# A layer step of a hybrid decoder: the last steps of the decode attention spread over the sixth weight product and into the next turn

## The chip, the core and the metric

The kernel runs on one core of a Trainium2 chip. The metric is the device time of one execution in microseconds (us), taken as the median of several runs. All products go through TensorE (PE in the profile); VectorE is DVE, ScalarE is ACT, GpSimd is POOL, and SyncE (SP) issues most DMAs. ACT issues some DMAs itself; its issuing part stands in rows as ACTq, and SP's as SPq.

## The reference, cut to what matters

One layer takes 512 prompt tokens and 8 x 8 new tokens of running sequences. A normalised input goes through one projection into two groups of heads: 8 attention heads of width 128 (sparse attention by an index; the new tokens also attend over 512 cached tokens per sequence, through paged `cache_k` and `cache_v`) and 16 state-space heads of width 64 (Mamba-2, which also updates a stored state per sequence). Output projection, residual, a gated feed-forward part and a final norm follow.

```python
def sparse_attend(q, k_sel, v_sel, idx, qpos, rel_bias):
    logits = jnp.einsum('bqhd,bqkhd->bqhk', q, k_sel).astype(jnp.float32) * (ATT_HEAD_DIM ** -0.5)
...
    p = jax.nn.softmax(logits, axis=-1)
    return jnp.einsum('bqhk,bqkhd->bqhd', p.astype(v_sel.dtype), v_sel)
...
    h_new = h * jnp.exp(last)[..., None, None] + jnp.einsum('bjh,bjhn,bjhp->bhpn', wts, Bc, xc)
...
    h = x + jnp.concatenate([att, y], axis=-1) @ w_out
```

The outputs are both groups' results after the layer, and also every new key, value, convolution tail and state.

## The kernel before, in words

Tokens lie along the free axis, 576 of them (512 prompt, 64 decode), in two halves of 288 columns. Every weight product is done in three passes (activation high part times weight high part, low times high, high times low), 16 k-tiles of 6 matmuls. Half of such a product (8 k-tiles, 48 matmuls) reads one 8-tile half of a weight unit. ACT makes the high part of the weights (`WH`, line 730 in the turns), POOL the low part (`WL`, line 734).

The middle of the program is a row of nine "turns" (`turn_pe`, `turn_act`, `turn_dve`, `turn_sp`, one per engine, each with the turn's number i). Turn i does at once: the q, k and v products of head i (six half products, `product(i, 0)` to `product(i, 5)`; i up to 7), the state-space work of head pair i (i up to 7), and the attention of head a = i - 1 (i from 1 to 8). The order on each engine is the order of the code; nothing is scheduled. Turn 8 has only attention. All small results pass through four PSUM banks, and the list `turn` gives the order in which names use each bank: whoever writes a name first waits (`tclaim`) until the name before it in the same bank has been taken out (`ttaken`).

The pieces of a turn that the change touches are these. Prompt attention: `qk0` to `qk3` are the logits of the four query blocks (DVE `logits`, ACT `exp_logits`, DVE `normal`), `pt0` to `pt3` the transposed probabilities (copied by ACT to the two halves of the tile `pt`), `pv0` to `pv3` the values (`values`, copied by ACT to `attT`). Decode attention: `lnew` are the logits over the new tokens, `S` those over the cache; `lgs` holds both, with number 4 in `exp_logits` and `normal`. The probabilities are transposed (`pts`, and in it the part `ptn` for the new tokens), `pvs` are the values over the cache `vca` (64 matmuls), DVE joins them to `attS`, PE transposes this (`ats`), ACT puts it into `attT`, and a DMA stores `attT` to the scratch `mixS` (semaphore `mixa`). State space: `xtok`, `btok`, `cb`, `su`, `y0` to `y3`, `ys`, then `us0` and `us1`, which update the decode state `h0` in place on DVE, and `fin`, the final prompt state. ACT stores `fin` (`ssm_prompt`), the head's output `xs` (`mixS`) and `h0` (`ssm_sample`, semaphore `hout`).

SP loads the inputs of the next turn's state-space work in `load_mamba(i + 1)`: eleven DMAs (`xs`, `bf`, `cf`, `sz`, twice `ea`, `abc`, `dcol`, and last the state `h0`), into the same tiles. It waits for the stores of turn i first, and PE waits for all eleven:

```python
                        sp.wait_ge(s["hout"], 16 * i + 16)
                        sp.wait_ge(s["link_s"], 4 * i + 4)
                        load_mamba(i + 1)
...
                    pe.wait_ge(s["ssm_in"], LOADS * (i + 1))
                    by_token(i, "xtok", xs)
```

After turn 8 the output projection begins; its loads wait for all stores to `mixS`. Time in a turn is counted below from the start of `product(i, 0)` at line 802 of PE.

## Time and profile before

| what | value |
|---|---|
| median of three runs | 3050.3 us (3049.33 to 3051.59) |
| the profiled execution's own time | 3047.6 us |
| its span, first to last instruction | 3045.6 us |
| PE busy | 2827.9 us, 93% of the span |
| DVE, ACT, POOL busy | 1509.6, 952.2, 548.0 us |
| mean granted clock of TensorE | 0.965 |

The span is divided by engine and line; a row of the timeline gives the start in us, the duration, the engine, the line, the operation, output and inputs, and in brackets how long the engine had been idle before it and who released it. The turns with products lie between about 575 and 1151 us, turn 8 between 1151 and 1208 us. Overlapping rows are normal on PE, where matmuls are pipelined.

### The profile page before, as it was taken

What the parts mean: (1) busy time and instruction counts of PE and PEld (TensorE: products, weight loads), DVE (VectorE), ACT (ScalarE), POOL (GpSimd) and SP (SyncE); (2) the same over time, 40 slices, a digit from 0 to 9 for tenths busy, and PEclk for the clock granted to TensorE, in tenths of its full rate; (3) what the DMA queues carried; (4) which work ended last, traced back from release to release, by engine and by line L of the source; (5) the groups of instructions that cost most, each with busy time, mean ns of one, the idle gap of its engine ahead of it and who ended that gap; (6) DMA issues with size and microseconds to landing.
All of it is one profiled execution on the core that took longest, in us unless ns stands there. A gap on an engine that the chain in (4) does not pass through costs nothing.

```text
span 3045.6 us, 49651 instructions
## 1 busy us (share of the span) xinstructions
PE 2827.9 (93%) x20713; PEld 2688.3 (88%) x20713; DVE 1509.6 (50%) x2311; ACT 952.2 (31%) x1442; POOL 548.0 (18%) x230
## 2 busy tenths in 40 slices
PE   6999999689999996997799999999999999999997
PEld 5887898577777773997799999999999999999997
DVE  3312599444444443213767667676766733222323
ACT  4223222133333322323443434334343322121222
POOL 1222233111111110332000000000000033333331
PEclk8999999799999997998899999999999999999999
DMA  6422231455555545433123233332323352323221
GB/s 201 119 67 77 68 106 50 126 145 145 152 148 152 151 139 169 140 127 104 64 94 124 99 119 100 108 112 97 127 99 107 127 198 99 114 99 115 99 99 63
DMA packets 367372, 354.00 MB, mean 116 GB/s; under 512 B 40957, under 2 KB 321125, under 8 KB 365880
## 3 DMA queue, kind: packets, MB, share of 16 engines
q1 hardware_dynamic: 334136, 325.20, 33.7%
q10 hardware_dynamic: 33024, 25.77, 2.6%
q8 instruction: 158, 2.59, 0.3%
q14 instruction: 54, 0.44, 0.0%
HBM read 303.18 MB, written 49.13 MB: 116 GB/s over the span
## 4 chain that ended last, share of the span: by engine, by line
PE 57%; issue 32%; POOL 7%; DVE 2%; ACTq 1%; ACT 1%; POOLq 0%; DVEq 0%
PE PS L1242 32%; PE PS L1224 18%; PE PS L802 6%; POOL WL L705 4%; POOL WL L734 3%; ACTq L1286 0%; DVE XR L2282 0%; ACTq L1287 0%; DVE xo_t L2287 0%; DVE xo_x L2287 0%; DVE y_out L2357 0%; POOL WL L726 0%; ACT WRAW L1295 0%; DVE rstd L2275 0%; PE PS L817 0%
## 5 line engine op out<-in xcount | busy, mean ns | idle before, releaser
L802 PE MATMUL PS<-AH,WH 128*128 128x288 f32 (+1 forms) x2208 | 493.5, 306 | 21.0 <-DVE AL L2184 7.3
L1224 PE MATMUL PS<-H,WH 128*128 128x288 f32 x2816 | 489.5, 296 | 0.7 <-DVE us L2249 0.7
L802 PE MATMUL PS<-AL,WH 128*128 128x288 f32 (+1 forms) x2208 | 481.1, 300 | 0.0
L802 PE MATMUL PS<-AH,WL 128*128 128x288 f32 (+1 forms) x2208 | 480.1, 299 | 0.0
L724 POOL TENSOR_TENSOR WL<-WRAW,WH 128x1024 fp32r<-128x1024 f32 x88 | 213.8, 2430 | 1378.8 <-ACT WH L717 1378.8
L1224 PEld LDWEIGHTS PS<-H,WH 128*128 128x128 f32 x2816 | 414.4, 189 | 0.9 <-issue 0.9
L802 PEld LDWEIGHTS PS<-AH,WH 128*128 128x128 f32 (+1 forms) x2208 | 363.6, 193 | 44.9 <-issue 28.9
L1242 PE MATMUL PS<-xo_t,WH 128*128 128x288 f32 x1888 | 380.1, 296 | 8.6 <-ACT kept L1643 7.5
L802 PEld LDWEIGHTS PS<-AL,WH 128*128 128x128 f32 (+1 forms) x2208 | 363.9, 193 | 0.0
L802 PEld LDWEIGHTS PS<-AH,WL 128*128 128x128 f32 (+1 forms) x2208 | 363.1, 192 | 0.0
L2343 DVE TENSOR_TENSOR XD<-PS,XD 128x576 f32<-128x576 f32 x176 | 133.4, 758 | 398.8 <-PE PS L1224 398.8
L1242 PEld LDWEIGHTS PS<-xo_t,WH 128*128 128x128 f32 x1888 | 303.6, 188 | 9.0 <-issue 9.0
L1224 PE MATMUL PS<-H,WL 128*128 128x288 f32 x1408 | 301.5, 296 | 0.0
L1242 PE MATMUL PS<-xo_x,WH 128*128 128x288 f32 x1408 | 285.4, 297 | 14.3 <-DVE xo_x L2287 14.3
L1242 PE MATMUL PS<-xo_t,WL 128*128 128x288 f32 x944 | 278.4, 295 | 0.0
L2200 DVE TENSOR_TENSOR WL<-WRAW,WH 128x1024 fp32r<-128x1024 f32 x147 | 179.9, 1224 | 126.8 <-ACT WH L1635 126.8
L1242 PEld LDWEIGHTS PS<-xo_x,WH 128*128 128x128 f32 x1408 | 227.7, 190 | 14.7 <-DVE xo_x L2287 14.7
L717 ACT CAST WH<-WRAW 128x1024 fp32r<-128x1024 f32 x88 | 92.7, 1054 | 435.5 <-PE PS L1224 430.7
L1224 PEld LDWEIGHTS PS<-H,WL 128*128 128x128 f32 x1408 | 226.9, 189 | 0.0
L1242 PE MATMUL PS<-xo_x,WL 128*128 128x288 f32 x704 | 208.3, 296 | 0.0
L1242 PE MATMUL PS<-xo_t,W 128*128 128x288 f32 x1392 | 196.0, 297 | 10.4 <-DVE xo_t L2287 10.4
L705 POOL TENSOR_TENSOR WL<-WRAW,WH 128x1024 fp32r<-128x1024 f32 (+1 forms) x58 | 139.4, 2406 | 361.3 <-ACT WH L700 361.3
(353 smaller groups left out, 3796.2 us busy)
## 6 DMA issues: line engine op xcount, KB each, us to landing
WRAW<-in_w_gate SPq DMA_DIRECT2D x22, 2048.0 KB
WRAW<-in_w_up SPq DMA_DIRECT2D x22, 2048.0 KB
WRAW<-in_w_down SPq DMA_DIRECT2D x22, 2048.0 KB
WRAW<-in_w_in SPq DMA_DIRECT2D x14, 2048.0 KB, 8.4
raw<-in_w_in SPq DMA_DIRECT2D x48, 512.0 KB, 4.1
kca<-in_cache_k SPq DMA_DIRECT2D x256, 64.0 KB, 2.8
vca<-in_cache_v SPq DMA_DIRECT2D x256, 64.0 KB, 2.0
WRAW<-in_w_out SPq DMA_DIRECT2D x16, 1024.0 KB
```

The source lines that it names most:

```text
L705: nc.gpsimd.tensor_tensor(WL[:, half, :, 0:w], raw[:, 8 * half:8 * half + 8, :], WH[:, half, :, 0:w].bitcast(F32), ALU.subtract).then_inc( ...
L717: nc.scalar.copy(as_down(WH, h % 2), w_down_half((1, 0)[f % 2], h)).then_inc(s["w_hi"], 1)
L724: nc.gpsimd.tensor_tensor(as_down(WL, h % 2), w_down_half((1, 0)[f % 2], h), as_down(WH, h % 2).bitcast(F32), ALU.subtract).then_inc(s["w_ ...
L734: nc.gpsimd.tensor_tensor(WL[:, half, :, :], raw, WH[:, half, :, :].bitcast(F32), ALU.subtract).then_inc(s["w_lo"], 1)
L802: last = nc.tensor.matmul(G[gslot][0:width, h, 0:HALF], wt[:, half, k % 8, 0:width], act[:, (k + shift) % KT, h * HALF:(h + 1) * HALF], st ...
L1224: last = mm(G[(slot + t) % 2][:, h, 0:HALF], wt[:, half, 2 * k + t, :], hid[:, m, k, h * HALF:(h + 1) * HALF], start=(k == 0 and wt is WH ...
L1242: last = mm(out, wt[:, k, :], act[:, m, k, :], start=(j in (0, 1, 3) and k == 0 and wt is wh and m == 0), stop=(k == 7 and wt is wl), skip ...
L2200: tt(w_low(r), operand(up, j, r), w_high(r).bitcast(F32), ALU.subtract).then_inc(s["p_lo"], 1)
L2343: tt(two(XD[:, n, :]), G[n % 2][:, :, 0:HALF], two(XD[:, n, :]), ALU.add).then_inc(s["tile_taken"], 1)
```

## The change

The change reorders work in the turns; no instruction's size or type changes, and the count of instructions stays the same but for waits.

On PE, the small steps that stood together in the middle of `product(i, 5)` (before k-tile 12) are cut into four parts, before k-tiles 9, 11, 13 and 15. The transposes of the decode probabilities (`pts`, and now `ptn` in a bank of its own) join the last part. After the product come `pvs` and then `values(i, 3)`. The transpose `ats` moves into the next turn, behind its `product(i, 0)`; the last one has a bank use of its own, `ats_last`. `qk1` moves behind `product(i, 0)`, `qk3` behind `xtok`, and `lnew` behind `product(i, 1)`. On ACT, `exp_logits(i, 4)` comes before the copy of `pt2`; the copies of `pts` and `ptn` and the three state-space stores (now `mamba_out`) come before the copy of `pv3`; the end of the attention (now `store_att`) follows `exp_logits(i, 1)` of the next turn. On DVE, `normal(i, 4)` stands between the updates from `us0` and `us1`, and the work on `lnew` (now `new_keys`) behind `take(i, 0, qT)`. SP's order is the same.

```diff
-        turn = [("qk0", 0), ("qk1", 1), ("qk2", 0), ("qk3", 1), ("lnew", 0), ("xtok0", 2), ("xtok1", 3), ("btok0", 2), ("btok1", 3),
+        turn = [("qk0", 0), ("qk1", 1), ("ats", 3), ("qk2", 0), ("qk3", 1), ("lnew", 0), ("xtok0", 2), ("xtok1", 3), ("btok0", 2), ("btok1", 3),
                 ("ktok0", 1), ("ktok1", 0), ("cb0", 2), ("cb1", 3), ("kca0", 0), ("kca1", 1), ("su", 3), ("S", 2), ("kca2", 0), ("hTb0", 3),
                 ("kca3", 1), ("y0", 3), ("kca4", 0), ("hTb1", 3), ("kca5", 1), ("y1", 3), ("vtok0", 0), ("vtok1", 1), ("y2", 3),
                 ("kca6", 0), ("y3", 3), ("kca7", 1), ("pt0", 0), ("ys", 3), ("pt1", 0), ("pv0", 1), ("us0", 3), ("pt2", 0), ("pv1", 1), ("us1", 2),
-                ("pt3", 0), ("pv2", 1), ("fin", 3), ("pv3", 1), ("pts", 0), ("pvs", 1), ("ats", 0)]
+                ("pt3", 0), ("pv2", 1), ("fin", 3), ("pts", 0), ("ptn", 2), ("pvs", 1), ("pv3", 1)]
...
-            def product(i, n, mid=None):
+            def product(i, n, between=None):
 
                 if n % 2 == 0:
                     pe.wait_ge(s["tile_taken"], 3 * i + (28 + n // 2))
-                half_unit(pe, 6 * i + 58 + n, n % 2, (1, 0, 1)[n // 2], ready=(lambda k: mid() if k == 12 else None) if mid else None)
+                half_unit(pe, 6 * i + 58 + n, n % 2, (1, 0, 1)[n // 2], ready=(lambda k: between[k]() if k in between else None) if between else None)
...
-                    qk(i, 1)
                 if units:
                     product(i, 0)
                     if early:
@@ -1044,18 +1044,24 @@
                             product(i, n)
                         pe.wait_ge(s["h_init"], 4)
                 if att:
+                    qk(i, 1)
+                    if i >= 2:
+                        tclaim(pe, "ats", i)
+                        back_att(i, "ats")
                     qk(i, 2)
+                if mamba:
+                    pe.wait_ge(s["ssm_in"], LOADS * (i + 1))
+                    by_token(i, "xtok", xs)
+                if att:
                     qk(i, 3)
+                if units and not early:
+                    product(i, 1)
+                if att:
                     tclaim(pe, "lnew", i)
                     pe.wait_ge(s["qpad_done"], a + 1)
                     for m in range(2):
                         last = mm(bank("lnew")[:, 0:NS], qpad[:, 4 * m:4 * m + 4, :].rearrange("p b r -> p (b r)"), kT[:, NP:NT], start=(m == 0), stop=(m == 1))
...
-                def rest():
+                def rest0():
                     if att:
                         probs_t(i, 1)
                         values(i, 0)
                     if mamba:
                         update(i, 0)
+
+                def rest1():
                     if att:
                         probs_t(i, 2)
                         values(i, 1)
                     if mamba:
                         update(i, 1)
+
+                def rest2():
                     if att:
                         probs_t(i, 3)
                         values(i, 2)
+
+                def rest3():
                     if mamba:
                         tclaim(pe, "fin", i)
                         pe.wait_ge(s["hT_done"], 4 * i + 4)
                         tmade(tr(bank("fin")[:, 0:P], hT[:, 3, :], ident[:, :]), "fin")
                     if att:
-                        values(i, 3)
+                        tclaim(pe, "pts", i)
+                        pe.wait_ge(s["prob"], 5 * a + 5)
+                        for j in range(4):
+                            last = tr(bank("pts")[:, j * P:(j + 1) * P], lgs[:, j * P:(j + 1) * P], ident[:, :])
+                        tmade(last, "pts")
+                        tclaim(pe, "ptn", i)
+                        tmade(tr(bank("ptn")[0:NS, 0:P], lgs[:, NP:NT], ident[:, :]), "ptn")
                 if units:
-                    product(i, 5, rest)
+                    product(i, 5, {9: rest0, 11: rest1, 13: rest2, 15: rest3})
                 else:
-                    rest()
-                if att:
-                    tclaim(pe, "pts", i)
+                    for part in (rest0, rest1, rest2, rest3):
+                        part()
+                if att:
                     tclaim(pe, "pvs", i)
-                    pe.wait_ge(s["prob"], 5 * a + 5)
+                    tgiven(pe, "pts", i)
+                    tgiven(pe, "ptn", i)
+                    pe.wait_ge(s["vca_in"], 512 * a + 512)
                     out = bank("pvs")
-                    for j in range(4):
-                        tr(bank("pts")[:, j * P:(j + 1) * P], lgs[:, j * P:(j + 1) * P], ident[:, :])
-                    last = tr(out[0:NS, 3 * P:4 * P], lgs[:, NP:NT], ident[:, :])
-                    tmade(last, "pts")
-                    tgiven(pe, "pts", i)
-                    pe.wait_ge(s["vca_in"], 512 * a + 512)
                     for m in range(2):
                         mm(out[:, m * P:(m + 1) * P], ptn[:, :], vtok[0:NS, 4, :], start=True, stop=False)
                         for j in range(4):
                             for c in range(4):
                                 last = mm(out[32 * c:32 * c + 32, m * P:(m + 1) * P], pts[:, j, 32 * c:32 * c + 32], vca[:, 4 * m + c, j, :], start=False, stop=(j == 3))
                     tmade(last, "pvs")
-                    tclaim(pe, "ats", i)
-                    pe.wait_ge(s["att_s"], a + 1)
-                    tmade(tr(bank("ats")[:, 0:P], attS[:, :], ident[:, :]), "ats")
+                    values(i, 3)
+
+            def back_att(i, name):
+
+                pe.wait_ge(s["att_s"], i - 1)
+                tmade(tr(B[3][:, 0:P], attS[:, :], ident[:, :]), "ats")
...
+            def store_att(a):
+
+                ttaken(copy(attT[:, NP:NT].rearrange("p (m c q) -> p m c q", m=2, c=4), B[3][:, 0:P].rearrange("p (c m q) -> p m c q", c=4, m=4)[:, 0:2, :, :]), "ats")
+                if a < 7:
+                    tgiven(act, "ats", a + 2)
+                else:
+                    given(act, "ats_last")
+                act.dma_start(bass.AP(mixS.tensor, a * (P * NT), [[NT, P], [1, NT]]), attT[:, :]).then_inc(s["mixa"], 16)
+
+            def mamba_out(i):
+
+                tgiven(act, "fin", i)
+                act.dma_start(bass.AP(O["ssm_prompt"].tensor, i * (P * P), [[P, P], [1, P]]), fin).then_inc(s["finout"], 16)
+                act.wait_ge(s["y_done"], i + 1)
+                act.dma_start(bass.AP(mixS.tensor, i * (P * NT) + 8 * P * NT, [[NT, P], [1, NT]]), xs[:, :]).then_inc(s["ymix"], 16)
+                act.wait_ge(s["h_done"], 2 * i + 2)
+                act.dma_start(bass.AP(O["ssm_sample"].tensor, i * (P * P), [[P, P], [NM * DS * P, NB], [1, P]]), h0[:, :, :]).then_inc(s["hout"], 16)
...
+                    if i >= 2:
+                        twait(act, "ats", i)
+                        store_att(a - 1)
...
+                        if t == 2:
+                            exp_logits(i, 4)
                         evac(i, f"pt{t}", pt[:, t % 2, 0:(t + 1) * P], bank(f"pt{t}")[:, 0:(t + 1) * P])
+                        if t == 3:
+                            evac(i, "pts", pt[:, 0, :], bank("pts")[:, :])
+                            evac(i, "ptn", ptn[:, :], bank("ptn")[0:NS, 0:P])
+                            if mamba:
+                                mamba_out(i)
                         evac(i, f"pv{t}", attT[:, t * P:(t + 1) * P], bank(f"pv{t}")[:, 0:P])
                         if t == 2 and mamba:
                             if later:
                                 act.wait_ge(s["finout"], 16 * i)
                             evac(i, "fin", fin, bank("fin")[:, 0:P])
...
+                def new_keys():
+
...
+                if att:
+                    new_keys()
...
+                        if att and g == 0:
+                            normal(i, 4)
```

The order of PE's instructions at the end of a turn and the start of the next, before (names as in the code; `lg` and `lgs` are the prompt and decode probabilities, and rows of the weight products have AH and WH):

```order
L1188 MATMUL PS<-pt,vtok 128x128 x2
L1143 MATMUL PS<-ident,hT 128x128 [waits hT_done,free3]
L1188 MATMUL PS<-pt,vtok 128x128 [waits free0,free1]
L1188 MATMUL PS<-pt,vtok 128x128 x3
L802 MATMUL PS<-AH,WH 128x288 x2
...
L1156 MATMUL PS<-ident,lgs 128x128 [waits prob,free1,free0]
L1156 MATMUL PS<-ident,lgs 128x128 x3
L1157 MATMUL PS<-ident,lgs 64x128
L1162 MATMUL PS<-vtok,ptn 128x128 [waits vca_in,free0]
...
L1169 MATMUL PS<-ident,attS 128x128 [waits att_s,free0]
L968 MATMUL PS<-kT,qT 128x128 [waits free0,tile_taken]
L968 MATMUL PS<-kT,qT 128x256 [waits free1]
```

and the same place in the change:

```order
L1205 MATMUL PS<-pt,vtok 128x128 x2
L803 MATMUL PS<-AH,WH 128x288 x2
...
L1155 MATMUL PS<-ident,hT 128x128 [waits hT_done,free3]
L1160 MATMUL PS<-ident,lgs 128x128 [waits prob,free0]
L1160 MATMUL PS<-ident,lgs 128x128 x3
L1163 MATMUL PS<-ident,lgs 64x128 [waits free2]
L803 MATMUL PS<-AH,WH 128x288 x2
...
L1176 MATMUL PS<-vtok,ptn 128x128 [waits free2,vca_in,free0,free1]
...
L1205 MATMUL PS<-pt,vtok 128x128 [waits free0,free1]
L1205 MATMUL PS<-pt,vtok 128x128 x3
L969 MATMUL PS<-kT,qT 128x128 [waits free0,tile_taken]
```

Where `fin` (`hT`) stood with four k-tiles of the product behind it, it now has one, and so have the transposes of `lgs`.

ACT at the end of a turn, from the copy of `pt2` on, before:

```order
L1442 COPY pt<-PS 128x384 [waits full0,full1]
L1442 COPY attT<-PS 128x128 [waits full1]
L1442 COPY cbm<-PS 128x128 [waits full3,finout]
L1442 COPY pt<-PS 128x512 [waits full0,full1]
L1442 COPY attT<-PS 128x128 [waits full1]
L1563 DMA ssm_prompt<-cbm 128x128 [waits free3]
L1565 DMA mixS<-xs 128x576 [waits y_done]
L1452 ACTIVATE lgs,stat<-lgs,stat 128x576 [waits nmax]
L1570 DMA ssm_sample<-h_108 128x8x128 [waits h_done]
L1573 COPY ptn<-PS 64x128 [waits full0]
L1574 COPY pt<-PS 128x512
L1442 COPY attT<-PS 128x64 [waits full0]
```

and in the change:

```order
L1471 ACTIVATE lgs,stat<-lgs,stat 128x576 [waits nmax,full1]
L1461 COPY pt<-PS 128x384 [waits full0]
L1461 COPY attT<-PS 128x128 [waits full1]
L1461 COPY cbm<-PS 128x128 [waits full3,finout]
L1461 COPY pt<-PS 128x512 [waits full0,full1]
L1461 COPY pt<-PS 128x512 [waits full0]
L1461 COPY ptn<-PS 64x128 [waits full2]
L1502 DMA ssm_prompt<-cbm 128x128 [waits free3]
L1504 DMA mixS<-xs 128x576 [waits y_done]
L1506 DMA ssm_sample<-h_108 128x8x128 [waits h_done]
L1461 COPY attT<-PS 128x128 [waits full1]
```

The three stores stood behind the copy of `pv3` and stand behind the copies of `pts` and `ptn` now, which wait for PE's last part.

PE between `product(i, 0)` and `product(i, 1)`, before:

```order
L968 MATMUL PS<-kT,qT 128x384 [waits free0]
L968 MATMUL PS<-kT,qT 128x512 [waits free1]
L1052 MATMUL PS<-kT,qpad 128x64 [waits qpad_done,free0]
L1052 MATMUL PS<-kT,qpad 128x64
L977 MATMUL PS<-ident,xs 128x128 [waits free3,free2,ssm_in]
L977 MATMUL PS<-ident,xs 128x128 x3
L979 MATMUL PS<-ident,xs 64x128
```

and in the change:

```order
L969 MATMUL PS<-kT,qT 128x256 [waits free1]
L1186 MATMUL PS<-ident,attS 128x128 [waits att_s,free3]
L969 MATMUL PS<-kT,qT 128x384 [waits free0]
L978 MATMUL PS<-ident,xs 128x128 [waits free3,free2,ssm_in]
L978 MATMUL PS<-ident,xs 128x128 x3
L980 MATMUL PS<-ident,xs 64x128
L969 MATMUL PS<-kT,qT 128x512 [waits free1]
```

`qk1` and `ats` are new ahead of `xtok` (the rows with `xs`), `qk3` (128x512) is behind it, and `ats` uses bank 3 just before `xtok` does.

## Rows read from the trace of the kernel before

**Rows 1.** PE's waits over the whole run: total us, times, longest.

```profile
PE PS L1169 <- DVE stat L2161: 9.1, 8, 1.1
PE PS L1066 <- ACT btok L1442: 4.6, 8, 0.6
```

**Rows 2.** Timeline of PE, end of turn 6 and start of turn 7.

```profile
1052.08 0.85 PE L802 MATMUL PS<-AH,WH 128*128 128x288 f32 x2
...
1061.10 0.27 PE L1143 MATMUL PS<-ident,hT 128*128 128x128 f32 x1
1062.37 1.13 PE L1188 MATMUL PS<-pt,vtok 128*128 128x128 f32 x8 [0.99 <-ACT pt L1442]
1063.26 0.51 PE L802 MATMUL PS<-AH,WH 128*128 128x288 f32 x2
...
1066.52 0.60 PE L1156 MATMUL PS<-ident,lgs 128*128 128x128 f32 x4
...
1068.06 0.48 PE L1162 MATMUL PS<-vtok,ptn 64*128 64x128 f32 x2 [0.83 <-ACT pt L1574]
...
1072.81 0.89 PE L968 MATMUL PS<-kT,qT 128*128 128x128 f32 x4 [0.39 <-ACT attT L1442]
1073.36 0.61 PE L802 MATMUL PS<-AH,WH 128*128 128x288 f32 x2
```

**Rows 3.** Timeline of ACT, its issues of stores at the ends of turns 0 and 6.

```profile
594.12 0.44 ACTq L1570 DMA_DIRECT2D ssm_sample<-h  x1
...
1063.54 0.35 ACTq L1563 DMA_DIRECT2D ssm_prompt<-cbm  x1
...
1064.47 0.39 ACTq L1570 DMA_DIRECT2D ssm_sample<-h  x1
...
1067.27 0.26 ACT L1573 COPY ptn<-PS 64x128 f32<-64x128 f32 x1 [1.97 <-PE PS L1157]
```

**Rows 4.** SP: its longest wait for a DMA, and its issues after turn 6.

```profile
SPq L558 <- DMA ssm_sample<-h: 168.8, 7, 30.2
1068.16 0.33 SPq L508 DMA_DIRECT2D xs<-xcS  x1
...
1073.65 0.61 SPq L516 DMA_DIRECT2D h<-in_state_ssm  x1
```

**Rows 5.** The load of the state after turn 6, from its issue to its landing.

```profile
DMA to landing us min/median/max: 6.9/6.9/6.9
```

**Rows 6.** Timeline of PE in turn 7, from product 0 to product 1's end.

```profile
1079.92 1.66 PE L968 MATMUL PS<-kT,qT 128*128 128x384 f32 x4
1081.42 0.61 PE L1052 MATMUL PS<-kT,qpad 128*128 128x64 f32 x4
1081.87 0.60 PE L977 MATMUL PS<-ident,xs 128*128 128x128 f32 x4
...
1088.80 0.60 PE L977 MATMUL PS<-ident,bf 128*128 128x128 f32 x4
```

**Rows 7.** Timeline of DVE in turn 7, behind product 1.

```profile
1086.25 0.21 DVE L2071 SCALAR_TENSOR_TENSOR lgs<-PS,neg_s 128x64 f32<-128x64 f32 x1
...
1090.39 2.43 DVE L2032 TENSOR_SCALAR lg<-lg,stat 128x512 f32<-128x512 f32 x1
```

**Rows 8.** PE in turn 1, and the windows view: busy us, PEclk, DMA.

```profile
610.40 0.95 PE L977 MATMUL PS<-ident,xs 128*128 128x128 f32 x4 [4.11 <-DMA h<-in_state_ssm]
...
618.96 0.60 PE L977 MATMUL PS<-ident,bf 128*128 128x128 f32 x4
610.62:614.03 3.41, 3.41 (x17) 3.37 (x16) 1.84 (x7) 2.69 (x9) 0.00 (x0) 0.50 0.85 214
```

**Rows 9.** Turn 8: logits 1 on DVE and ACT, and the last store.

```profile
1158.34 0.41 DVE L2019 SCALAR_TENSOR_TENSOR lg<-PS,neg_p 128x256 f32<-128x256 f32 x1
...
1160.12 0.19 ACT L1452 ACTIVATION_READ_ACCUMULATOR lg<-lg,stat 128x1 f32 x1
...
1208.17 0.35 ACTq L1578 DMA_DIRECT2D mixS<-attT  x1
```

More of the change, by code:

```diff
@@ L315, in nth @@
                 return first[b] + in_mamba[name]
-            if isinstance(i, int) and i == 8:
-                return first[b] + n_mamba[b] + 7 * n_all[b] + extra[b] + in_att[name]
-            return n_all[b] * i + (first[b] + n_mamba[b] - n_all[b] + in_turn[name])
+            if i == 8:
+                return first[b] + n_mamba[b] + 7 * n_all[b] + extra[b] + in_att[name] - (b == 3)
+            return n_all[b] * i + (first[b] + n_mamba[b] - n_all[b] + in_turn[name]) - (b == 3)
         first, extra = list(count), [0, 0, 1, 1]
         for b in range(4):
-            count[b] = first[b] + n_mamba[b] + 7 * n_all[b]
+            count[b] = first[b] + n_mamba[b] + 7 * n_all[b] - (b == 3)
         plan("ssy0", 2)
@@ L327, in build @@
             count[b] += n_att[b]
+        plan("ats_last", 3)
         plan("ssf0", 2)
@@ L1053, in turn_pe @@
                     tmade(last, "lnew")
-                if mamba:
-                    pe.wait_ge(s["ssm_in"], LOADS * (i + 1))
-                    by_token(i, "xtok", xs)
-                if units and not early:
-                    product(i, 1)
                 if mamba:
@@ L1200, in _ @@
             turn_pe(8, units=False, mamba=False)
+            claim(pe, "ats_last")
+            back_att(9, "ats_last")
             def norm_sum():
@@ L1556, in turn_act @@
                             evac(i, "fin", fin, bank("fin")[:, 0:P])
-                if mamba:
-                    if not att:
-                        if later:
-                            act.wait_ge(s["finout"], 16 * i)
-                        evac(i, "fin", fin, bank("fin")[:, 0:P])
-                    tgiven(act, "fin", i)
-                    act.dma_start(bass.AP(O["ssm_prompt"].tensor, i * (P * P), [[P, P], [1, P]]), fin).then_inc(s["finout"], 16)
-                    act.wait_ge(s["y_done"], i + 1)
-                    act.dma_start(bass.AP(mixS.tensor, i * (P * NT) + 8 * P * NT, [[NT, P], [1, NT]]), xs[:, :]).then_inc(s["ymix"], 16)
-                if att:
-                    exp_logits(i, 4)
-                if mamba:
-                    act.wait_ge(s["h_done"], 2 * i + 2)
-                    act.dma_start(bass.AP(O["ssm_sample"].tensor, i * (P * P), [[P, P], [NM * DS * P, NB], [1, P]]), h0[:, :, :]).then_inc(s["hout"], 16)
-                if att:
-                    twait(act, "pts", i)
-                    copy(ptn[:, :], bank("pvs")[0:NS, 3 * P:4 * P])
-                    ttaken(copy(pt[:, 0, :], bank("pts")[:, :]), "pts")
-                    evac(i, "ats", attT[:, NP:NT].rearrange("p (m c q) -> p m c q", m=2, c=4),
-                         bank("ats")[:, 0:P].rearrange("p (c m q) -> p m c q", c=4, m=4)[:, 0:2, :, :])
-                    tgiven(act, "ats", i)
-                    act.dma_start(bass.AP(mixS.tensor, a * (P * NT), [[NT, P], [1, NT]]), attT[:, :]).then_inc(s["mixa"], 16)
+                if mamba and not att:
+                    if later:
+                        act.wait_ge(s["finout"], 16 * i)
+                    evac(i, "fin", fin, bank("fin")[:, 0:P])
+                    mamba_out(i)
             turn_act(0, att=False)
@@ L1587, in _ @@
             turn_act(8, units=False, mamba=False)
+            wait(act, "ats_last")
+            store_att(7)
             def hi_p(c, h, f, down=False):
@@ L2150, in turn_dve @@
                     ls.end()
-                if att:
+                if att and not mamba:
                     normal(i, 4)
```

## The prediction

> **What bounds the kernel now.** I read the granted clock first, then PE's waits, then the timeline of one turn on PE, ACT, DVE and SP. In the turns PE has few idle places, each short and each recurring once a turn: PE waits for DVE before the transpose of `attS` (9.1 us in 8 times), and for ACT's copy of `btok` (4.6 us in 8 times) [rows 1]. The end of turn 6 holds most of it [rows 2]: 0.99 before `pv3`, 0.83 before `pvs`, 1.14 before `ats` (9.1 / 8) and 0.39 before `qk0`, 3.35 us. The change aims at these. From the start of product 0 in turn 6 to that in turn 7 a turn takes some 78 us.
>
> The second reading is who comes just behind PE. The state-space inputs of the next turn go a long way round: ACT issues the store of `h0` at 1064.47 [rows 3], SP waits for its landing (line 558, 168.8 us in 7 turns, its only long DMA wait here), begins the eleven loads at 1068.16 and issues the last one at 1073.65 [rows 4], and that lands 6.9 us later [rows 5], at 1080.55. PE's `xtok` starts at 1081.87 [rows 6]. So from the issue of the store to the last landing it is 16.1 us, and the slack is 1.3 us. In turn 1 there is none: issue at 594.12 [rows 3], `xtok` at 610.40 after 4.11 us of idle PE [rows 8], 16.3 us. The loads are what PE meets next if it gets faster or they get later; the change does both.
>
> **The change part by part, with turn 6 to 7 as the model.** Product 5 starts at 1052.08 and `fin` at 1061.10 [rows 2], 9.0 later, with four k-tiles ahead of it. Four k-tiles at full clock take 3.26 (1063.26 to 1066.52), 0.81 each. Now seven are ahead of `fin`: 3 x 0.81 = 2.4 more, so `fin` starts at 1063.5. Behind it the copies of `fin` and `pt3` come on ACT, and `pts` needs the bank of `pt3`, as `pv3` did: 1.27 later (1061.10 to 1062.37), so `pts` starts at 1064.8. That idle 0.99 stays, in a new place. `pts` and `ptn` take some 0.65, k-tile 15 covers the 0.83 that `pvs` waited for, `pvs` starts at 1066.3 and takes 2.9 (1068.06 to 1072.81 less 1.14, 0.39 and the transpose 0.3), `pv3` 0.9, `qk0` 0.2: product 0 at 1070.3 instead of 1073.36, 3.1 us earlier. That is the gain.
>
> The stores. Before, they were issued when the copy of `pv3` began, from 1063.54 to 1064.47, 0.93 from first to last [rows 3]. Now they follow the copies of `pts` and `ptn`. In the old order the first such copy began 0.75 after `pts` on PE (1066.52 [rows 2], 1067.27 [rows 3]) and waited for both; now `pts` is copied first, so the second copy begins at about 0.9: 1065.7, and the `h0` store is issued at 1066.65, 2.2 us later. The landing chain of 16.1 makes the last load land at 1082.75. SP's queue has nothing else that waits there; the K loads behind `load_mamba` move with it and are not needed before product 1 is done, so I cost them at nothing.
>
> PE reaches `xtok` after product 0 (6.56, 1073.36 to 1079.92), `qk1` 0.35, `ats` 0.15 and `qk2` 0.65: at 1078.0. It waits 4.8 us. So the 3.1 us are lost in this wait, and `xtok` comes 0.9 later than before (2.2 less the slack 1.3). `store_att` on ACT costs nothing while this wait covers it.
>
> Behind `xtok` the loop has become longer. `qk3` stood ahead of it, beside the load, and is now behind: `qk2` and `qk3` take 1.50 (1079.92 to 1081.42 [rows 6]), four of seven blocks are `qk3`'s, 0.86. `lnew` (0.45, from 1081.42 to 1081.87) goes behind product 1, where PE waited 0.59 for `btok` [rows 1]: nothing. But its work on DVE moves too. The two instructions from 1086.25 on took 0.5 [rows 7] in a place with slack. Now they stand ahead of `normal(i, 2)` and `normal(i, 3)`, of which the second was held until POOL's pass ended (2.43 us at 1090.39 for work that takes 0.5). In the new order the first is held and the second comes after it; the mask of `cb`, on which `su` and product 2 depend, comes 0.65 later. Bounds: 0 (if the order still fits) to 1.1; I take 0.65.
>
> The clock. Turn 1 shows what a long wait at `xtok` brings: the granted clock was 0.50 from 610.62 for 3.41 us [rows 8], its lower level of 1.2 GHz, after PE had been idle 4.11 us. From `xtok` to the end of product 1 it took 8.56 (610.40 to 618.96), against 6.93 (1081.87 to 1088.80 [rows 6]) without: 1.6 us. With a wait of 4.8 in every turn I expect that each time, but part of the low stretch may fall into the wait itself. Bounds 0 and 1.6, possibly twice that; I take 1.2.
>
> Sum, against the profiled execution's own 3047.6. Turn 0: `fin` has three more k-tiles ahead, so the first chain starts 2.4 later, and `xtok` of turn 1 waits for it already: +2.4. Turn 1 to 2: 0.9 + 0.86 + 0.65 = +2.4 (its wait and low clock are in the old time). Turns 2 to 6: 5 x (0.9 + 0.86 + 0.65 + 1.2) = 5 x 3.6 = +18.0. Turn 7: 0.86 + 0.65 + 1.2 behind `xtok`, and then the early end at last counts, -3.1: -0.4. Turn 8: the last store of attention (1208.17 [rows 9]) no longer stands behind `pv3` and its copy and an exp that waited for it, but `pv3` now sits before the last `ats`: 1 to 3 less, I take 1.8. Total +20.6: 3068. The profiled run lies 2.7 below the median of the runs, so the median becomes 3071.
>
> **Rivals.** (1) The forecast, late stores that hold `xtok`, with low clock: 3071, chance 0.6, its own range 3060 to 3082. (2) The same wait, but the clock stays up and DVE loses nothing: 6 x 1.2 + 7 x 0.65 = 11.8 less, 3059, chance 0.2. For it: idle places of 1 us at the end of turns cost no clock; against: turn 1. (3) Faster: the loads come in time, because the chain is shorter when it runs under a quieter time (`mixS` from `attT` no longer runs beside it). The point is 13.1 us instead of 16.1: then `xtok` is held by something else, bank 3, which `ats` uses just ahead and ACT empties only behind `exp_logits(i, 1)`. On DVE and ACT that took 1158.34 to 1160.31, 2.0 [rows 9], so `xtok` comes at 6.9 + 2.0 + 0.5 = 9.4 after product 0's start instead of 8.5. Per turn then 0.9 + 0.86 + 0.65 - 3.1 = -0.7, six times, turn 1 -2.5 at its end and -3 at its wait, turn 8 -1.8: -11.5, 3039. Turn 0's chain had no `attT` store beside it and still took 16.3, so 0.08. (4) The gain and the lateness cancel, 3050: it needs a chain some 2.5 us shorter, 0.07. (5) The low clock lasts twice as long after each wait: another 10, 3081, 0.05.
>
> The Trainium skill (DMA: Bandwidth & Descriptors, Anatomy of one DMA) fits a DMA as 2.0 us plus its bytes at 436 GB/s, for GpSimd's path. As an estimate from that page, the store of 0.52 MB would take 3.2 us and the 2.6 MB of loads 7.9, a chain of 11.1 us, and then rival (3) would hold with 3039; the trace does not agree, since its loads alone take 12.4 (1068.16 to 1080.55).
>
> **How the numbers follow.** A measurement of this kernel tells about 0.2% (6 us) from no change. Slower are (1), (2) and (5): 0.85; the same (4): 0.07; faster (3): 0.08. The range leaves out (3), (4) and the far end of (5): 3053 to 3083.
>
> **What would show it.** In the changed profile: PE waits at `xtok` for the load of `h` in every turn from 1 to 7, 4 to 6 us in turns 2 to 7; the store of `h0` is issued 14.5 after product 5 starts instead of 12.4; product 0 starts 3 us earlier relative to product 5; a clock of 0.50 right behind each wait; from one `xtok` to the next 81.5 to 82.5 us; the waits before `ats`, `pvs` and `qk0` are gone, and about 1 us is left before `pts`. I am wrong if the eleven loads land within 13 us of the store's issue, or if ACT issues the stores as early as before.

## The result: slower by 0.86%

The changed kernel took 3078.2 us in the median of four runs (3072.7 to 3079.6), the kernel before 3051.0 (3049.3 to 3052.9) beside it: a ratio of 1.0086, 95% interval 1.0068 to 1.0103. In a later comparison on another chip (e13 below) the ratio was 1.0087 (1.0074 to 1.0101). The forecast was 3071 in a range of 3053 to 3083. The execution profiled after took 3079.6 us (span 3077.5, mean granted clock 0.960), 32.0 more than the one before (3047.6, clock 0.965); the spans differ by 31.9.

PE's waits over the whole run, after (total us, times, longest):

```profile
PE PS L978 <- DMA h<-in_state_ssm: 30.3, 7, 9.3
...
PE PS L1085 <- DVE cbm L2135: 7.8, 8, 1.0
PE PS L1160 <- ACT pt L1461: 7.3, 8, 1.1
...
PE PS L1205 <- DVE attS L2197: 6.9, 8, 0.9
```

The first row is new: 30.3 us of waits at `xtok` for the load of the state, once in each of turns 1 to 7. Of the four small waits of [rows 2] the first stays, now before `pts` (line 1160); the other three are gone, and a new one has come, before `pv3` (line 1205). The row of line 1085 is the wait before `su` for DVE's mask of `cb`; it was 4.2 us before.

PE's timeline in the changed kernel, from product 5 of turn 6 to `xtok` of turn 7:

```profile
1081.58 0.63 PE L1198 MATMUL PS<-ident,lg 128*128 128x128 f32 x2
...
1092.00 0.27 PE L1155 MATMUL PS<-ident,hT 128*128 128x128 f32 x1
1093.17 0.65 PE L1160 MATMUL PS<-ident,lgs 128*128 128x128 f32 x4 [0.90 <-ACT pt L1461]
...
1098.61 1.16 PE L1205 MATMUL PS<-pt,vtok 128*128 128x128 f32 x8 [0.86 <-DVE attS L2197]
1099.60 0.39 PE L969 MATMUL PS<-kT,qT 128*128 128x128 f32 x2
...
1106.74 0.81 PE L969 MATMUL PS<-kT,qT 128*128 128x384 f32 x2
1111.02 0.90 PE L978 MATMUL PS<-ident,xs 128*128 128x128 f32 x3 [3.46 <-DMA h<-in_state_ssm]
```

ACT's store of the state, and SP's first and last load behind it:

```profile
1094.85 0.45 ACTq L1506 DMA_DIRECT2D ssm_sample<-h  x1
```

```profile
1099.02 0.33 SPq L509 DMA_DIRECT2D xs<-xcS  x1
...
1104.26 0.59 SPq L517 DMA_DIRECT2D h<-in_state_ssm  x1
```

The last load lands at 1110.97, 16.1 us after the issue of the store, as in [rows 3 to 6], and `xtok` starts at 1111.02. Before, `xtok` of this turn came 1.3 us after the last landing (0.7 to 1.6 over turns 2 to 7); now it comes with it.

`xtok` of turns 4, 5 and 6 after, and what each waited:

```profile
865.99 1.11 PE L978 MATMUL PS<-ident,xs 128*128 128x128 f32 x4 [3.80 <-DMA h<-in_state_ssm]
...
948.67 1.12 PE L978 MATMUL PS<-ident,xs 128*128 128x128 f32 x4 [4.48 <-DMA h<-in_state_ssm]
...
1029.26 1.11 PE L978 MATMUL PS<-ident,xs 128*128 128x128 f32 x4 [2.91 <-DMA h<-in_state_ssm]
```

From `xtok` to `xtok` that is 82.7 and 80.6; from turn 1 (619.33) to turn 7 (1111.02) it is 491.7 in six turns, 81.95 each. Before it was 78.6 ((1081.87 - 610.40) / 6, [rows 6, 8]). The loop adds up: from `xtok` to the issue of the store it is 65.85 us in the mean of turns 1 to 6, and from there to the next `xtok` 16.1.

Where the 31.9 us are lost, by the start of `xtok`: 8.9 by turn 1 (619.33 against 610.40), 20.2 from there to turn 7 (29.15 in all), 2.8 behind it. Turn 1's `xtok`, and the store of turn 0 that it waited for:

```profile
619.33 0.90 PE L978 MATMUL PS<-ident,xs 128*128 128x128 f32 x3 [9.31 <-DMA h<-in_state_ssm]
```

```profile
601.55 0.45 ACTq L1506 DMA_DIRECT2D ssm_sample<-h  x1
```

### The profile page after: what moved, and what is told of

Read it like the earlier page. It is cut to its first block, busy times and chain, and to the rows that moved or that the text cites. A ratio compares the mean times of both kernels' runs of the same rounds, so it can differ in the third digit from the quotient of the medians.

```text
span 3077.5 us, 49659 instructions
## 1 busy us (share of the span) xinstructions
PE 2843.4 (92%) x20713; PEld 2698.6 (88%) x20713; DVE 1485.3 (48%) x2311; ACT 951.0 (31%) x1442; POOL 547.5 (18%) x230
## 4 chain that ended last, share of the span: by engine, by line
PE 56%; issue 33%; POOL 7%; DVE 2%; ACTq 1%; ACT 1%; POOLq 0%; DVEq 0%
PE PS L1261 32%; PE PS L1243 18%; PE PS L803 6%; POOL WL L706 4%; POOL WL L735 3%; ACTq L1305 0%; DVE XR L2321 0%; ACTq L1306 0%; DVE xo_t L2326 0%; DVE xo_x L2326 0%; DVE y_out L2396 0%; POOL WL L727 0%; ACT WRAW L1314 0%; DVE rstd L2314 0%; PE PS L818 0%
## 5 line engine op out<-in xcount | busy, mean ns | idle before, releaser
L803 PE MATMUL PS<-AH,WH 128*128 128x288 f32 (+1 forms) x2208 | 501.1, 309 | 22.3 <-DVE AL L2223 7.2
L735 POOL TENSOR_TENSOR WL<-raw,WH 128x1024 fp32r<-128x1024 f32 x48 | 113.5, 2365 | 531.7 <-ACT WH L731 531.7
```

Source lines behind the costliest of these rows:

```text
L735: nc.gpsimd.tensor_tensor(WL[:, half, :, :], raw, WH[:, half, :, :].bitcast(F32), ALU.subtract).then_inc(s["w_lo"], 1)
L803: last = nc.tensor.matmul(G[gslot][0:width, h, 0:HALF], wt[:, half, k % 8, 0:width], act[:, (k + shift) % KT, h * HALF:(h + 1) * HALF], st ...
```

## The experiments

All ratios are to the kernel before on the same chip, with 95% intervals; five rounds each.

**e13, the changed kernel again.**

> The changed kernel unaltered, on the chip of these runs, as the yardstick for the runs on it: 3078 as before if its waits repeat (ratio 1.007 to 1.010); if the phase of the low clock decides which turns wait long, single runs scatter between 3068 and 3082.

Measured: 3077.6 us (3073.1 to 3080.8), ratio 1.0087 (1.0074 to 1.0101), waits at `xtok` again 30.3 us. The size of the loss repeats; it is the yardstick below.

**e1, the state's load taken off xtok's wait.**

```diff
-        LOADS = 16 * 11
+        LOADS = 16 * 10
...
                         sp.wait_ge(s["ymix"], 16 * i + 16)
-                        sp.wait_ge(s["hout"], 16 * i + 16)
                         sp.wait_ge(s["link_s"], 4 * i + 4)
                         load_mamba(i + 1)
+                        sp.wait_ge(s["hout"], 16 * i + 16)
+                        load_h(i + 1)
...
                 tclaim(pe, f"hTb{g}", i)
+                if g == 0:
+                    pe.wait_ge(s["h0_in"], 16 * (i + 1))
```

> The changed kernel with one wait taken apart: the state load h has a count of its own, which only the first transposes of h wait for, and the ten other loads of the next head no longer wait for the state's store. xtok then waits for neither. My theory (the chain store, state load holds xtok: 30.3 us of waits, and low clock behind them): the waits of L978 for the h load are gone, what is left of them is under 5 us in all; the time falls by 28 to 38 us, to 3040 to 3050. Rival (the loss is in the split of product 5 and in what follows xtok, the wait only takes the place of other waits): waits show up elsewhere, the time stays at 3065 or above.

Measured: 3054.4 us, ratio 1.0005 (0.9992 to 1.0017), 0.8% or some 25 us less than the changed kernel. The chain is the cause of nearly all of the loss. The edit does two things, and they were not parted: the state has a count of its own, and the ten other loads no longer queue behind the store. In the changed kernel the last of the ten, `dcol`, landed at 1108.92, 5.2 us after its issue and 2.05 before the state. So the count alone would spare `xtok` of turn 7 about 2.1 of its 3.46 us, an estimate from these two landings.

```profile
1103.74 0.48 SPq L516 DMA_DIRECT2D dcol<-in_d_skip  x1
```

The time only comes back to that of before, above what I expected. A wait for the loads is left in turn 1 alone (4.3 us), and another has taken the place of the rest. PE's waits in e1:

```profile
PE PS L984 <- ACT attT L1500: 9.0, 6, 1.5
```

`xtok` now waits 1.5 us for bank 3, which `ats` has used and ACT empties behind `exp_logits(i, 1)`: the next limit that the forecast's third rival named.

**e6, the same separation in the kernel before.** Edit as in e1.

> The kernel before with the state load h on a count of its own, as in the run e1_state_apart on the changed one. In the kernel before the load lands 0.2 to 1.7 us ahead of xtok, so that nothing waits for it. My theory: no change, 3050 within 0.2%, xtok to xtok 78.3 us as before. Rival (the chain bounds the kernel before too, by work that is placed behind it): 3040 or less.

Measured: 3051.5 us, ratio 0.9995 (0.9984 to 1.0006). Only turn 1 of the kernel before met the chain: its wait of 4.1 us is 0.55 in e6. That is too little to show in the time. The separation pays where the store comes late in every turn.

**e5, the kernel before with only the store late.**

```diff
-                if mamba:
-                    act.wait_ge(s["h_done"], 2 * i + 2)
-                    act.dma_start(bass.AP(O["ssm_sample"].tensor, i * (P * P), [[P, P], [NM * DS * P, NB], [1, P]]), h0[:, :, :]).then_inc(s["hout"], 16)
                 if att:
                     twait(act, "pts", i)
                     copy(ptn[:, :], bank("pvs")[0:NS, 3 * P:4 * P])
                     ttaken(copy(pt[:, 0, :], bank("pts")[:, :]), "pts")
+                if mamba:
+                    act.wait_ge(s["h_done"], 2 * i + 2)
+                    act.dma_start(bass.AP(O["ssm_sample"].tensor, i * (P * P), [[P, P], [NM * DS * P, NB], [1, P]]), h0[:, :, :]).then_inc(s["hout"], 16)
```

> The kernel before with one thing moved: the state store of turns 1 to 6 is issued behind ScalarE's copies ptn and pt, about 3.1 us later (1067.6 instead of 1064.47 in turn 6); the tail of the turn stays as it was. My theory (the chain store, state load is the bound as soon as its slack of 1.3 us is used): PE waits 1.5 to 3 us for the h load at xtok of turns 2 to 7, a low clock behind some of them; 6 turns by 1.9 to 3.1 makes 3061 to 3069. Rival (the state load is hidden and what costs in the changed kernel is its new order on PE and VectorE): no such waits, 3050 within 0.2%.

Measured: 3061.7 us against 3049.7, ratio 1.0042 (1.0029 to 1.0055). PE's waits in e5:

```profile
PE PS L977 <- DMA h<-in_state_ssm: 12.1, 7, 4.4
```

The median rose by 12 us for a late store alone, with nothing moved on PE or DVE: the rival that blamed their new order falls for this part, and the lateness is enough by itself to cost time, here about half of the changed kernel's loss. The 12.1 of the row is another sum: 4.4 of it are turn 1's, which waited 4.1 before, and turns 2 to 7 waited 1.0 to 1.6 each, 7.7 together, less than the 1.5 to 3 expected. The profiled execution (3054.0) is also the fastest of the five, so its rows do not account for all of the 12 us.

**e4, the stores early in the changed kernel.**

```diff
                     if att:
                         probs_t(i, 3)
+                    if mamba:
+                        tclaim(pe, "fin", i)
+                        pe.wait_ge(s["hT_done"], 4 * i + 4)
+                        tmade(tr(bank("fin")[:, 0:P], hT[:, 3, :], ident[:, :]), "fin")
+                    if att:
                         values(i, 2)
...
                         if t == 3:
+                            if mamba:
+                                mamba_out(i)
                             evac(i, "pts", pt[:, 0, :], bank("pts")[:, :])
                             evac(i, "ptn", ptn[:, :], bank("ptn")[0:NS, 0:P])
-                            if mamba:
-                                mamba_out(i)
```

> The changed kernel with the final-state transpose put between pt3 and pv2 (step 13 instead of 15 of product 5), and ScalarE's three stores right behind the pt3 copy, ahead of the pts and ptn copies. My theory (each us by which the state store is issued sooner is a us less of waiting at xtok, until the slack is there): the store leaves 1.5 to 3 us sooner, the waits of turns 2 to 7 fall from 3.5 to 0.5 to 2 us, low clock behind them goes, the time falls by 10 to 25 us, to 3054 to 3068. Rival (ScalarE's issue of three stores, 1.2 us, now delays the pts copy, and pvs waits instead): 3075 or above.

Measured: 3050.8 us, ratio 1.0000 (0.9984 to 1.0017), 0.86% less than the changed kernel. The waits in e4:

```profile
PE PS L978 <- DMA h<-in_state_ssm: 12.4, 5, 5.5
```

They fall from 30.3 to 12.4, of which 5.5 are turn 1's; in two turns `xtok` waits 1.5 us for bank 3 instead. The wait before `pts` is gone too: ACT still copies `fin` and then `pt3`, but two k-tiles of the product now run on PE between `fin` and `pts` and cover both copies. So e4 by itself would not show that the chain was the cause, since it shortens the turn's end as well. e1 leaves that end as it is and gives back the same amount; the lateness of the store against the chain is what both edits remove.

**e3, qk3 ahead of xtok again.**

```diff
                     qk(i, 2)
+                    qk(i, 3)
                 if mamba:
                     pe.wait_ge(s["ssm_in"], LOADS * (i + 1))
                     by_token(i, "xtok", xs)
-                if att:
-                    qk(i, 3)
                 if units and not early:
```

> The changed kernel with the 128x512 logits product qk3 back ahead of xtok, where PE waits anyway for the h load. My theory (xtok's start is set by the load, so 0.86 us of work put into the wait comes off behind it, in each of turns 1 to 7): the waits of L978 fall by about 0.86 each, the time by 4 to 6 us, to 3072 to 3074. Rival (the work behind xtok is not what sets the way from xtok to product 5, DVE or the loads are): under 1.5 us, 3077 or above.

Measured: 3061.1 us, ratio 1.0036 (1.0023 to 1.0049). That is 0.5% or 15 us less than the changed kernel, where I expected 4 to 6. Two turns, from `xtok` to `xtok` (busy us of PE, PEld, DVE, ACT, POOL, then PEclk); first the changed kernel, then e3:

```profile
865.99:948.67 82.68, 72.92 (x545) 61.64 (x545) 32.81 (x91) 24.38 (x60) 14.84 (x7) 0.95 0.51 144
```

```profile
779.00:857.01 78.01, 70.28 (x545) 59.46 (x545) 33.60 (x92) 24.18 (x60) 13.88 (x7) 1.00 0.56 157
```

The turn of e3 has no stretch of low clock, though its `xtok` still waited 2.65 us:

```profile
857.01 0.66 PE L978 MATMUL PS<-ident,xs 128*128 128x128 f32 x4 [2.65 <-DMA h<-in_state_ssm]
```

Three of e3's turns 2 to 7 (3, 4 and 6) have no low stretch around `xtok`; in the changed kernel all six have one. That the shorter idle time is why the clock stayed up was not tried by itself, and its length alone does not decide it: 2.91 us came with a low stretch in turn 6 of the changed kernel, 2.94 us with none in turn 3 of e3.

**e2, product 5 of turn 0 whole.**

```diff
-                if units:
+                if early:
+                    product(i, 5, {12: lambda: (rest0(), rest1(), rest2(), rest3())})
+                elif units:
                     product(i, 5, {9: rest0, 11: rest1, 13: rest2, 15: rest3})
```

> The changed kernel with product 5 of turn 0 as before: its state updates and the final transpose all at step 12, not at 9, 11 and 15. My theory (in turn 0 the early pieces cost product 5 its clock for 13.65 us instead of 3.41 and put the first state store 5 us later than forecast): the first store is issued at about 596.5 instead of 601.55, the wait of turn 1 falls from 9.3 to about 4 us, and the time falls by 4 to 6 us, to 3073. Rival (the low clock in turn 0 has another cause, or turn 1 waits for another link): within 1 us of 3078.

Measured: 3068.9 us, ratio 1.0054 (1.0035 to 1.0074), 8 to 10 us less than the changed kernel. The first store left at 592.3, expected 596.5. `xtok` of turn 1 started at 608.2 in its profile, against 619.3 (and 614.6 in e13's). The direction is shown by both; the size is more than expected, and executions differ in how long the clock is low in turn 0 (13.65 us in one of the changed kernel, 6.83 in the other, and not at all in product 5 of e2's).

**e8, e1 with the old order ahead of xtok.** As e1, and `qk3` and `lnew` ahead of `xtok`, `new_keys` ahead of DVE's wait for the loads.

> The run e1_state_apart (changed kernel, xtok not waiting for the state) with the products qk3 and lnew back ahead of xtok, and VectorE's new_keys back ahead of its wait for the loads, as in the kernel before. It prices the moved pieces apart from any wait. My theory: xtok to the y_decode products shrinks from 46.13 us to 44.75 (0.86 of qk3, 0.65 of VectorE's order), qk0 to xtok grows from 9.46 to 10.4, so that a turn gains about 0.4 to 0.6 us and the time 3 to 5 us against e1_state_apart. Rival (VectorE's order costs nothing, what lies between is all PE's own work and only changes sides): xtok to xtok stays at 78.35.

Measured: 3047.6 us, ratio 0.9995 (0.9986 to 1.0004), not told apart from e1. `xtok` to `ys` (the products of `y_decode`) took 44.75 us instead of 46.13, but `qk0` to `xtok` 10.8 instead of 9.5. PE's row ahead of `xtok` in e8:

```profile
923.99 0.66 PE L1064 MATMUL PS<-kT,qpad 128*128 128x64 f32 x4 [1.47 <-DVE lg L2057]
```

The rival's number was right: `xtok` to `xtok` took 78.17 to 78.52 us in five of e8's six turns, as in e1. Without the load's wait the moved pieces only change sides, and `lnew` waits 1.5 us for a bank where `xtok` waited 1.5 for another. Their 1.4 us cost something only while a load sets `xtok`'s start, since what stands ahead of it is then free. Its reason was not right: DVE's order does cost, as the wait before `su` for DVE's mask shows, in e3 (new order) and in e8 (old order):

```profile
PE PS L1084 <- DVE cbm L2134: 7.8, 8, 1.0
```

```profile
PE PS L1091 <- DVE cbm L2142: 4.1, 8, 0.5
```

**e9, both cures** (e1 and e4).

> The changed kernel with both cures: the state load on a count of its own (e1_state_apart) and the final-state transpose and the three stores earlier (e4_stores_early). In the first the tail took 14.8 us at full clock and 16.3 with its low stretch, in the second 13.7 and 15.3. My theory: no wait at xtok, a turn of 75.7 us at full clock and of 77.3 with one low stretch of 3.41 us, against 78.3 in the kernel before: 7 turns by 1 to 2.6, less about 4 us lost in turns 0 and 1: 3036 to 3048. Rival (the low stretch comes once in 78.5 us whatever the turn holds, and the turn falls in step with it): a turn of 78.3 to 78.5 us, 3050 to 3054.

Measured: 3042.2 us, ratio 0.9972 (0.9960 to 0.9983): faster than the kernel before. Two turns of e9, one at full clock and one with a low stretch of 3.41 us:

```profile
1001.64:1077.31 75.67, 69.98 (x545) 59.57 (x546) 33.94 (x92) 23.99 (x59) 14.23 (x6) 1.00 0.57 160
924.40:1001.64 77.24, 71.55 (x546) 60.73 (x546) 34.04 (x92) 24.00 (x59) 14.23 (x6) 0.98 0.54 153
```

The same instructions take 1.57 us more: the price of one such stretch. The rival of a turn held at 78.3 to 78.5 us falls.

**e10, e9 with product 5 whole in every turn** (as in e2, for all turns; unlike the kernel before, `pts` also stands in the middle of the product).

> The run e9_apart_early (both cures) with product 5 of every turn split at step 12 alone, as in the kernel before, its four groups of attention and state work all in that place. It prices the split apart from the waits. Theory A (the split lets the copies of pt run under the product's steps): the waits for the copies ahead of the pv and pt pieces come back, 1 to 2.5 us per turn, 3047 to 3058. Theory B (the pieces cost TensorE its clock, and the split is what it pays for): waits come back but low stretches go, above all the one of 13.65 us in turn 0: 3040 or less.

Measured: 3047.0 us, ratio 0.9983 (0.9973 to 0.9992). Its interval overlaps e9's, so the split's worth isn't settled by the times. In its profile the wait before `pts` is back:

```profile
PE PS L1169 <- ACT pt L1470: 8.0, 8, 1.1
```

and from `ys` to `qk0` a turn takes 23.1 us, against 21.6 in e9, both with one low stretch: 1.5 us per turn, within theory A's 1 to 2.5. Of these some 10 us the ratios show 3.4. Turn 0 accounts for much of the rest: its low stretch in product 5 is 6.83 us in e10 and 13.65 in e9, as theory B had it, and `xtok` of turn 1 starts at 608.28 instead of 612.41, 4.1 us sooner. In the other turns the low stretches did not go.

**e11, e9 with ACT's copy of ats first.**

```diff
                     exp_logits(i, 0)
-                    exp_logits(i, 1)
                     if i >= 2:
                         twait(act, "ats", i)
                         store_att(a - 1)
+                    exp_logits(i, 1)
```

> The run e9_apart_early with ScalarE's copy of ats (and the attention store) put ahead of exp_logits 1 instead of behind it. With the state's load off its path xtok waits 1.50 us in each of turns 2 to 7 for bank 3, until that copy is made. My theory: these 9.0 us go, a turn takes 74.2 us at full clock, the time falls by 7 to 10 us to 3033 to 3036. Rival (exp_logits 1 comes later, or the loads of xs and bf are not there yet, and PE waits for these): 3040 to 3043.

Measured: 3031.2 us, ratio 0.9937 (0.9919 to 0.9955). That is 0.35% or some 11 us less than e9, expected 7 to 10. `xtok` no longer waits for `attT`, and turns 2 to 7 have no wait at `xtok` at all; from `qk0` to `xtok` they take 7.8 us instead of 9.45. The row of line 984 for `lgs` grows from 1.9 to 7.8, about 1 us a turn, at a later instruction of that line:

```profile
PE PS L984 <- DVE lgs L2115: 7.8, 7, 1.9
```

**e12, e11 with turn 0's product 5 whole** (the edit of e2).

> The run e11_ats_copy_first with product 5 of turn 0 split at step 12 alone, as in e2_turn0_whole. In e9_apart_early the turn 0 still has its 13.65 us at the low clock and xtok of turn 1 comes 4 us after that of the kernel before. My theory: 3 to 6 us less than e11_ats_copy_first. Rival (with the waits for the state gone, turn 0's tail has slack): within 1.5 us of e11_ats_copy_first.

Measured: 3025.7 us, ratio 0.9914 (0.9897 to 0.9930), the fastest version: 0.86% under the kernel before, 1.7% under the changed one. Its step to e11 (5.5 us) is as expected, but the intervals overlap. A turn of e12 at full clock, 74.7 us:

```profile
836.41:911.14 74.73, 69.70 (x547) 59.67 (x546) 34.70 (x92) 24.08 (x59) 14.23 (x6) 1.00 0.57 161
```

## Why the prediction was right, and where its terms were off

**The mechanism held.** The store of the state leaves later, the chain from its issue to the landing of the load is as long as before (15.4 to 17.7 us, mean 16.3; forecast 16.1), and PE waits for it at `xtok` in turns 1 to 7. e1 and e4 remove the loss, e5 makes some of it in the kernel before. A turn took 81.95 us in the mean, inside the 81.5 to 82.5 named. The sum was less good than the mechanism: +31.9 us between the profiles, forecast +20.6. Turn 0 brought 6.5 of the difference and the end 5.0.

**Turns 1 to 7** were to cost 2.4 + 18.0 = 20.4 us from `xtok` to `xtok`; it was 20.2. So close a sum is in part luck: the single turns grew by 1.9 to 4.5 us, and of the signs named, the wait of 4 to 6 us in turns 2 to 7 came in turn 5 alone.

**Turn 0 was mis-sized:** +8.9 up to `xtok` of turn 1 instead of +2.4. "`fin` has three more k-tiles ahead" counted them at full clock. The windows view of the changed kernel around them:

```profile
585.03:598.68 13.65, 13.53 (x45) 9.78 (x45) 6.91 (x17) 0.00 (x0) 0.68 (x1) 0.50 0.00 1
```

For 13.65 us the granted clock was 0.50, 1.2 GHz, with PE busy 13.53 of them; before it was low for 3.41 in that product. So `fin` came at 600.08 instead of 592.59 and the store at 601.55 instead of 594.12 [rows 3]. The chain was 1.5 us longer as well, 17.8. Over all profiles the stretch is 6.8 to 13.7 us where turn 0's product is split (eight kernels) and 0 to 6.8 where it is whole (six); e13's profile, with 6.83, lost 4.2 us by `xtok` of turn 1. The ranges touch, so the split makes a long stretch likelier and is not shown to be its only cause.

**The end was mis-sized:** +2.8 behind `xtok` of turn 7, where I had -0.4 and -1.8. From that `xtok` to `qk0` of turn 8 it was +1.4 and not -0.4; the -3.1 for the tail is the term behind it. Turn 8 was to gain 1.8 and lost 1.1: from `qk0` (1182.30, before 1151.77) to the last store of attention it took 57.5 us, against 56.4.

```profile
1239.76 0.34 ACTq L1497 DMA_DIRECT2D mixS<-attT  x1
```

The windows view of its two parts, up to `pt0` and from there to `ats`, first before, then changed:

```profile
1151.77:1188.54 36.77, 21.39 (x67) 10.04 (x66) 11.26 (x24) 11.40 (x23) 0.00 (x0) 0.66 0.36 103
1188.54:1207.45 18.91, 12.68 (x109) 8.05 (x108) 3.42 (x9) 4.56 (x13) 0.00 (x0) 0.77 0.72 238
```

```profile
1182.30:1220.13 37.83, 22.37 (x68) 11.09 (x67) 11.27 (x24) 11.27 (x24) 0.00 (x0) 0.59 0.35 99
1220.13:1239.15 19.02, 14.37 (x109) 9.57 (x108) 4.14 (x10) 4.29 (x12) 0.00 (x0) 0.65 0.76 241
```

In the second part PE's time without work fell from 6.2 us (18.91 - 12.68) to 4.65, near the forecast gain. But the granted clock was 0.65 instead of 0.77 there, and the same work took 1.7 us more. In the first it was 0.59 instead of 0.66, and the work, now with one `ats` in it, took 1.0 more. So the term left out the clock of turn 8; why it was lower in the changed kernel's execution was not tried. The last 0.4 us lie behind turn 8.

**The tail's gain of 3.1 us was twice too large.** From product 5's start (1079.97) to product 0's (1099.75) it took 19.8 us, against 21.3 before [rows 2]: 1.5. The step from `fin` to `pts` (1.17, forecast 1.27) and `ats`' departure were right; but `fin` came 12.0 behind product 5's start instead of 11.4, and I had missed that `pvs` and `pv3` share bank 1, so that `pv3`, now behind, waits 0.86 us until DVE has taken `pvs` (line 1205). In turns 1 to 6 this mattered nothing: a wait for the load ate the gain, whatever it was, so the total came out right with a wrong term. For the same reason the waits were 3.5 us (2.75 to 4.48) and not 4.8. Turn 7, with no load behind it, showed the miss.

**The store** was issued 14.9 us behind product 5's start in turn 6 (1079.97 to 1094.85), forecast 14.5, and 13.3 to 14.9 over turns 1 to 6.

**qk3 and DVE's order.** e3 and e8 part them: 0.82 us behind `xtok` for `qk3` (46.13 to 45.31; forecast 0.86), and 0.56 for `lnew` and DVE's order together (45.31 to 44.75; forecast 0.65 for DVE alone). The rows of e3 and e8 for the wait before `su` part these two: in turns 1 to 7 it is 1.04 us in e3 and 0.52 in e8, so 0.52 are DVE's and next to nothing `lnew`'s, as forecast.

**The clock** behind the waits was low as forecast, in part longer: 6.83 us in turns 3 to 5. In the windows view of the changed kernel:

```profile
946.84:953.67 6.83, 5.00 (x16) 3.93 (x17) 2.53 (x6) 2.46 (x9) 2.35 (x1) 0.50 0.98 276
1028.76:1032.17 3.41, 2.91 (x8) 1.83 (x9) 0.91 (x2) 2.71 (x8) 2.36 (x1) 0.50 1.05 302
```

From `xtok` to `ys` turns 3 to 5 took 48.5 to 48.8 us against 46.1 in e1, 2.4 to 2.7 more, but the low stretch that the tail had before, worth some 1.6, was gone in them: net about 1. Turns 6 and 7 took 1.4 more and kept the tail's stretch. Forecast was 1.2, by another way; that the net in turns 3 to 5 comes near it is luck.

**The rivals.** The second (no clock loss, 3059) fell with the windows above. The fifth (a low clock twice as long) came true by its row in turns 3 to 5, 6.83 us, but not by its price of 10 us, for the reason just given; the 3078 measured lie nearer to its 3081 than to my 3071 because of turn 0 and the end. The third (loads in time) needed a chain of 13.1 us and the fourth one some 2.5 us shorter; it was 16.3. What the third said of bank 3 turned out true in e1: 1.50 us. The Trainium skill (DMA: Bandwidth & Descriptors, Anatomy of one DMA) would put the store of 0.52 MB at 3.2 us, an estimate from its fit for another path; in the changed kernel the store of turn 6 took 4.0 from issue to landing (3.6 to 5.3 over all eight). That is near the page's fit; the eleven loads behind it (12.0 us from 1099.02 to the landing at 1110.97) are where the page's fit, 7.9 us as an estimate, falls short.

## What to carry to other kernels

When a change takes waits out of one engine, first measure the slack of the round trips through DMA that start in the same region, and count by how much their first link moves: here 0.7 to 1.6 us of slack was all the room there was, and a store that left 2.5 us later in turn 6 (0 to 3.5 in turns 1 to 5) cost more than three removed waits gave. A transfer that closes such a round trip should be counted on its own semaphore and waited for at its first use, and loads that do not need the store should not queue behind it. With this and the stores issued earlier, the reordering that lost 0.9% gained 0.3% (e9), and 0.9% with two further small moves (e12).

## What was not expected of the hardware

The granted clock fell for stretches of 3.41 us and longer (6.83, 10.24 and 13.65), once per turn in turns 3 to 7 of the kernel before (among them at 893.92, 972.43, 1050.93) and in turns 2 to 7 of e1. In e1 PE was busy through all of the stretch:

```profile
909.08:912.49 3.41, 3.41 (x13) 2.85 (x12) 3.31 (x6) 0.54 (x2) 0.00 (x0) 0.50 0.00 0
987.58:991.00 3.42, 3.42 (x13) 2.85 (x12) 3.32 (x6) 0.54 (x2) 0.00 (x0) 0.50 0.01 2
```

They lie in the small pieces around product 5. One of 3.41 us costs about 1.6 us, and some turns escape them: e12 had three full-clock turns of 74.7 us and one of 79.35 with 10.24 us at 0.50. The same kernel scatters by up to 24 us from run to run, more than some single edits here bring, and the mean granted clock goes with it in most: in e4 the fastest run (3038.5) had 0.970 and the slowest (3062.5) 0.959, in e12 3018.8 had 0.971 and 3034.0 0.963. In e8 it does not (3044.3 and 3052.6, both 0.965). So the clock is likely a large part of the scatter; what sets where it falls was not tried.
